# Banded attention: the sink as a score column, high parts of the memory weights on ScalarE, token-major sample values, and a third weight set for the output pair

## The reference, cut to what matters

```python
def sink_softmax(s, mask, sink):
    s = jnp.where(mask, s, -jnp.inf)
    sk = jnp.broadcast_to(sink.astype(jnp.float32), s.shape[:-1] + (1,))
    p = jax.nn.softmax(jnp.concatenate([s, sk], axis=-1), axis=-1)
    return p[..., :-1]
...
    s = jnp.einsum('nbqkgd,nbskd->nbkgqs', qb, kk, preferred_element_type=jnp.float32) * (HEAD_DIM ** -0.5)
...
    p = sink_softmax(s, mask[None, :, None, None], sink.reshape(KV_HEADS, GROUP)[None, None, :, :, None, None])
    o = jnp.einsum('nbkgqs,nbskd->nbqkgd', p.astype(vv.dtype), vv).reshape(n, t, Q_WIDTH)
...
def memory_kv(mem, g_mem, w_ck, w_cv):
    n, m = mem.shape[:2]
    mm = rmsnorm(mem, g_mem)
    mk = (mm @ w_ck).reshape(n, m, X_HEADS, X_HEAD_DIM)
    mv = (mm @ w_cv).reshape(n, m, X_HEADS, X_HEAD_DIM)
    return mk, mv
```

## Time and profile before

| | us |
|---|---|
| median of three timed runs | 2398.05 (2396.0 to 2401.09) |
| the profiled execution | 2398.91 |
| span of its trace | 2397.1 |
| mean granted TensorE clock | 0.981 |

### The profile page before, as it was taken

The page is one execution under the profiler, slowest core; times in us unless marked ns, Lnnn a source line. Parts: engine busy times, 40 slices in busy tenths (PEclk is TensorE's granted clock), DMA queues, the critical chain, the costliest instruction groups (busy, mean ns, idle before and its releaser), DMA issues.

```text
span 2397.1 us, 35513 instructions
## 1 busy us (share of the span) xinstructions
PE 2301.7 (96%) x14058; PEld 2066.1 (86%) x14058; DVE 1416.1 (59%) x1814; ACT 455.2 (19%) x924; POOL 1040.9 (43%) x703
## 2 busy tenths in 40 slices
PE   6999999999999999979899989999999999999997
PEld 5899989999989888867788967989999999999996
DVE  7755556555556677888525145375556565556565
ACT  5111000011000325345402034130000000000002
POOL 2643434343432256588354320535434343434333
PEclk9999999999999999989899999999999999999999
DMA  4201011101020211243311052122110111010102
GB/s 147 71 36 52 17 52 52 52 35 52 17 70 9 102 61 36 80 114 86 138 44 44 18 226 91 35 71 71 36 52 17 52 52 52 35 52 17 70 0 76
DMA packets 47781, 143.64 MB, mean 60 GB/s; under 512 B 7143, under 2 KB 17383, under 8 KB 45159
## 3 DMA queue, kind: packets, MB, share of 16 engines
q1 hardware_dynamic: 44768, 139.43, 16.8%
q10 hardware_dynamic: 2951, 3.35, 0.4%
HBM read 127.72 MB, written 12.26 MB: 58 GB/s over the span
## 4 chain that ended last, share of the span: by engine, by line
PE 88%; POOL 5%; DVE 3%; issue 2%; ACT 1%; DMA 0%; SPq 0%; POOLq 0%; ACTq 0%; DVEq 0%
PE ps L638 28%; PE ps L640 28%; PE ps L639 28%; PE ps L1088 1%; PE ps L1135 1%; POOL w_lo L534 1%; POOL kw_lo L534 1%; POOL w_hi L533 1%; POOL kw_hi L533 1%; PE ps L833 1%; DVE act_lo L1567 0%; POOL mix L591 0%; DVE y L2118 0%; PE ps L1095 0%; DMA x<-in_x 0%
## 5 line engine op out<-in xcount | busy, mean ns | idle before, releaser
L638 PE MATMUL ps<-act_hi,w_hi 128*128 128x288 f32 (+1 forms) x1968 | 658.5, 335 | 44.5 <-DVE act_lo L1567 23.6
L640 PE MATMUL ps<-act_hi,w_lo 128*128 128x288 f32 (+1 forms) x1968 | 650.6, 331 | 0.0
L639 PE MATMUL ps<-act_lo,w_hi 128*128 128x288 f32 (+1 forms) x1872 | 618.3, 330 | 0.0
L638 PEld LDWEIGHTS ps<-act_hi,w_hi 128*128 128x128 f32 x1968 | 375.2, 191 | 79.6 <-issue 44.3
L640 PEld LDWEIGHTS ps<-act_hi,w_lo 128*128 128x128 f32 x1968 | 375.4, 191 | 28.8
L639 PEld LDWEIGHTS ps<-act_lo,w_hi 128*128 128x128 f32 x1872 | 356.3, 190 | 28.8 <-issue 1.0
L1610 DVE SCALAR_TENSOR_TENSOR x<-ps,x 128x288 f32<-128x288 f32 (+1 forms) x504 | 263.4, 533 | 188.3 <-PE ps L640 173.0
L638 PE MATMUL ps<-hid_hi,dn_hi 128*128 128x288 f32 (+1 forms) x1056 | 347.5, 329 | 3.6 <-issue 3.6
L638 PE MATMUL ps<-act_hi,up_hi 128*128 128x288 f32 (+1 forms) x1056 | 347.7, 329 | 0.0
L639 PE MATMUL ps<-act_lo,up_hi 128*128 128x288 f32 (+1 forms) x1056 | 347.6, 329 | 0.0
L640 PE MATMUL ps<-act_hi,up_lo 128*128 128x288 f32 (+1 forms) x1056 | 347.6, 329 | 0.0
(11 more groups left out here) (264 smaller groups left out, 3021.8 us busy)
## 6 DMA issues: line engine op xcount, KB each, us to landing
w_raw<-in_w_ffn SPq DMA_DIRECT2D x66, 512.0 KB, 3.6
w_raw<-in_w_plain SPq DMA_DIRECT2D x54, 512.0 KB, 3.5
ff_raw_up<-in_w_ffn SPq DMA_DIRECT2D x44, 512.0 KB, 4.3
ff_raw_down<-in_w_ffn SPq DMA_DIRECT2D x22, 512.0 KB, 6.7
ck_T<-in_ck SPq DMA_DIRECT2D x8, 1024.0 KB, 7.0
cv_n<-in_cv SPq DMA_DIRECT2D x8, 1024.0 KB, 5.0
x_keep<-x SPq DMA_DIRECT2D x1, 4352.0 KB, 12.7
x<-x_keep SPq DMA_DIRECT2D x8, 544.0 KB, 5.2
```

What stands on the lines that cost most here:

```text
L638: pe.matmul(out, wh, ah, start=(first and n == 0), stop=False)
L639: pe.matmul(out, wh, al, start=False, stop=False)
L640: ins = pe.matmul(out, wl, ah, start=False, stop=end)
```

## The change

Six things are changed; what is computed stays the same.

1. The sink becomes column 257 of the scores (137 of the sample scores): set by a small copy (`set_sink`), it goes through the maximum and the exponentials with the others, and its share is in the sum. The separate exponential of the sink, the sum with it, and one step of the maxima go.
2. ScalarE makes the high parts of both slots for memory pairs from p = 2, and of slot 0 for p = 1 (`whi(p, s)`); GpSimd makes only low parts there.
3. The first memory pair: slot 0 is loaded before the wait for input tile 12 and split right behind the input pairs; slot 1 gets a set of its own (`kf_hi`/`kf_lo`), its load behind one swap load, and its product another PSUM bank. VectorE's third reciprocal of the recurrent group's norm moves behind the rotary of block 1.
4. The sample product gives token-major values: the weights are stationary in pieces of 32 columns and the values move. The result is copied by ScalarE (`so_T`) and turned back by TensorE in step 5 (`sample_back`); VectorE takes it in step 5, and the sample squares move from step 6 to 7.
5. The second output pair is split into a third set (`kx_hi`/`kx_lo`) when the last rotary and value transpose are done; the loop then covers pairs 2 and 3.
6. In the cross-attention the prompt product goes ahead of the sample product, with a semaphore of its own (`xp_ev`). ScalarE's `lru_hi` copies are spread over steps 5 and 6.

```diff
-        s_m = [here(f"s_m{s}", [P, NH, 2 * WIN]) for s in range(2)]
+        s_m = [here(f"s_m{s}", [P, NH, 2 * WIN + 1]) for s in range(2)]
...
+            def load_weights(p, s):
+                sp.wait_ge(w_split[s], p)
+                sp.dma_start(w_raw[s][:, :, :], pair_src(s, p)).then_inc(w_in[s], 16)
+
+            load_weights(PAIR_KV, 0)
             sp.wait_ge(lru_h, 4)
             sp.wait_ge(g_ev["in"], 6 + 13 * NC)
             load_swap(0)
+            load_weights(PAIR_KV, 1)
             load_swap(1)
-            load_pairs(PAIR_KV, PAIR_KV + 1)
             load_swap(2)
+            load_pairs(PAIR_KV + 1, PAIR_KV + 2)
...
-            split_pairs(1, PAIR_KV + 1, PAIR_IN, 0)
+            split_pairs(1, PAIR_KV, PAIR_IN, 0)
...
+            pool.wait_ge(w_mm[0], groups_before(PAIR_KV))
+            split_plain(0, PAIR_KV)
+            pool.wait_ge(ssq_mm, SUM0["lru"] + NC)
+            pool.wait_ge(lru_y, LT)
+            split_plain(1, PAIR_KV, [None, kf_hi], [None, kf_lo])
...
             for p in range(1, NB):
+                hi, lo = slots(kw_hi2[p % 2]), slots(kw_lo2[p % 2])
                 for s in range(2):
-                    if p == 1:
+                    if p == 1 and s == 1:
                         pool.wait_ge(w_mm[1], groups_before(PAIR_KV))
-                    elif s == 0:
-                        pool.wait_ge(kw_hi0, p - 1)
+                        split_plain(s, PAIR_KV + p, hi, lo, less=1)
                     else:
-                        pool.wait_ge(mem_mm, 2 * (p - 2) + 2)
-                    split_plain(s, PAIR_KV + p, p % 2, less=max(p - 1 - (s == 0), 0), both=p == 1 or s == 1)
+                        pool.wait_ge(kw_hi_made, 2 * (p - 1) + s if p > 1 else 1)
+                        split_plain(s, PAIR_KV + p, hi, lo, both=False)
...
+            pool.wait_ge(rope_done, NB)
+            pool.wait_ge(vt_mm, NB)
+            for s in range(2):
+                split_plain(s, PAIR_OUT + 1, slots(kx_hi), slots(kx_lo), less=less)
+            for s in range(2):
+                pool.wait_ge(w_mm[s], groups_before(PAIR_OUT + 1))
+                split_plain(s, PAIR_OUT + 2, less=less)
+            split_pairs(PAIR_OUT + 3, PAIRS, PAIR_OUT, 7 * NC, less=less)
...
-                for b in range(NS):
+                for h in range(2):
                     for kv in range(KVH):
-                        t, j = kv * 2 + b // 4, b % 4
-                        r = slice(kv * HD, kv * HD + HD)
-                        out = ps[r, 4, b * 32:(b + 1) * 32]
-                        pe.matmul(out, v_c[:, b, r], pcs_T[:, t, 32 * j:32 * j + 32], start=True, stop=False)
-                        ins = pe.matmul(out, vs_n[:, b, r], pns_T[:, t, 32 * j:32 * j + 32], start=False, stop=True)
+                        r, cols = slice(kv * HD, kv * HD + HD), slice(h * P + kv * HD, h * P + kv * HD + HD)
+                        for j in range(4):
+                            q = slice(32 * j, 32 * j + 32)
+                            pe.matmul(ps[q, 4, cols], pcs_T[:, kv * 2 + h, q], v_c[:, h * 4 + j, r], start=True, stop=False)
+                        for j in range(4):
+                            q = slice(32 * j, 32 * j + 32)
+                            ins = pe.matmul(ps[q, 4, cols], pns_T[:, kv * 2 + h, q], vs_n[:, h * 4 + j, r], start=False,
+                                            stop=True)
                 ins.then_inc(s_pv_mm, 1)
+
+            def sample_back():
+                pe.wait_ge(s_pt_ev, 4)
+                pe.wait_ge(pt_ev, 13)
+                for h in range(2):
+                    ins = pe.transpose(ps[:, 4, h * P:(h + 1) * P], so_T[:, h, :], ident[:, :])
+                ins.then_inc(s_back_mm, 1)
...
+            out_pair(1, kx_hi, kx_lo)
+            with pe.Fori(2, 4) as i:
+                out_pair(i, w_hi2, w_lo2)
...
             def x_weigh(b, half, s):
+                pe.wait_ge(xp_ev, b + 1)
+                pe.wait_ge(x_o_ev, b + 1)
+                for kt in range(KT):
...
-            def whi(p):
-
-                act.wait_ge(w_in[0], (PAIR_KV + p + 1) * 16)
-                act.wait_ge(mem_mm, 2 * (p - 2) + 2)
-                act.activation(kw_hi2[p % 2][:, 0, :, :], w_raw[0][:, :, :], ACT.Copy).then_inc(kw_hi0, 1)
+            def whi(p, s):
+
+                act.wait_ge(w_in[s], (PAIR_KV + p + 1) * 16)
+                if p == 1:
+                    act.wait_ge(w_mm[1], groups_before(PAIR_KV))
+                else:
+                    act.wait_ge(mem_mm, 2 * (p - 2) + 2)
+                act.activation(kw_hi2[p % 2][:, s, :, :], w_raw[s][:, :, :], ACT.Copy).then_inc(kw_hi_made, 1)
...
                 if b + 2 < NB:
-                    whi(b + 2)
+                    whi(b + 2, 0)
+                    whi(b + 2, 1)
...
+                if b == 4:
+                    act.wait_ge(s_pv_mm, 1)
+                    act.activation(so_T[:, :, :], ps[:, 4, 0:256], ACT.Copy).then_inc(s_pt_ev, 1)
...
                 steps.done(dve.tensor_reduce(st8[:, 0, :], scored(b)[:, :, :], AX_X, ALU.max))
-                steps.done(dve.scalar_tensor_tensor(out=st8[:, 1, :], in0=st8[:, 0, :], scalar=-(HD ** -0.5),
-                                                    in1=st8[:, 7, :], op0=ALU.mult, op1=ALU.min))
-                dve.tensor_tensor(st8[:, 2, :], st8[:, 1, :], c_("sink", 0, NH), ALU.add).then_inc(nmax_done, 1)
+                dve.tensor_scalar(st8[:, 1, :], st8[:, 0, :], -(HD ** -0.5), None, ALU.mult).then_inc(nmax_done, 1)
...
-                    steps.done(dve.tensor_tensor(st8[:, 5, h], st8[:, 3, h], st8[:, 4, h], ALU.add))
-                    steps.done(dve.reciprocal(st8[:, 6, h], st8[:, 5, h]))
+                    steps.done(dve.reciprocal(st8[:, 6, h], st8[:, 4, h]))
...
+            def set_sink(b, steps):
+                steps.done(dve.tensor_copy(scored(b)[:, :, 2 * WIN:2 * WIN + 1], st8[:, 7, :].unsqueeze(2)))
```

More of the change, by code:

```diff
@@ L230, in build @@
         vs_n = here("vs_n", [LS, NS, KVH * HD])
-        ss_m = here("ss_m", [P, 4, WIN + LS])
+        ss_m = here("ss_m", [P, 4, WIN + LS + 1])
         pcs_T = here("pcs_T", [P, 4, P])
         pns_T = here("pns_T", [LS, 4, P])
+        so_T = at("so_T", [P, 2, P], cur[0])
         qs_r = here("qs_r", [P, NS, GRP, LS])
@@ L564, in split_ffn, with split_plain @@
                 split_down(f, FI - 1)
-            def split_plain(s, p, v=0, less=0, both=True):
+            def split_plain(s, p, hi=w_hi, lo=w_lo, less=0, both=True):
                 pool.wait_ge(w_in[s], (p + 1) * 16)
                 steps = Steps(pool, w_pool, p * (2 * KT // SHORT) + s * (KT // SHORT) - less * (KT // SHORT))
-                split_short(w_raw[s], kw_hi2[v][:, s, :, :], kw_lo2[v][:, s, :, :], steps, w_split[s], both)
+                split_short(w_raw[s], hi[s], lo[s], steps, w_split[s], both)
             f = ffn["ffn1"]
@@ L1005, in block_step @@
                 if b == 5:
+                    pe.wait_ge(s_pt_ev, 4)
+                if b == 6:
                     pe.wait_ge(s_o_ev, 1)
@@ L1030, in block_step @@
                     sample_turn()
+                elif b == 5:
+                    sample_back()
                 if b + 2 < NB:
@@ L1064, in out_lo, with out_pair @@
                 return cat_lo[:, k, o:o + n] if k < LT else act_lo[:, k, o:o + n]
-            with pe.Fori(1, 4) as i:
+            def out_pair(i, hi, lo):
                 for s in range(2):
@@ L1124, in x_weigh @@
             def x_weigh(b, half, s):
+                pe.wait_ge(xp_ev, b + 1)
+                pe.wait_ge(x_o_ev, b + 1)
+                for kt in range(KT):
+                    for mt in range(2):
+                        ins = pe.matmul(ps[:, 6 + kt // 4, (kt % 4) * P:(kt % 4 + 1) * P],
+                                        mem_v[:, mt, kt * P:(kt + 1) * P], xp_T[:, mt, kt // 2, :],
+                                        start=(mt == 0), stop=(mt == 1))
+                ins.then_inc(x_pv_mm, 1)
                 pe.wait_ge(x_pt_ev, b + 2)
@@ L1937, in block_step @@
                     lru_lo(1)
+                if b + 2 < NB:
+                    set_sink(b + 2, steps)
                 if b + 1 < NB:
@@ L1962, in lru_inverse @@
                 dve.reciprocal(lru_rstd[:, o:o + n], lru_rstd[:, o:o + n]).then_inc(rstd_done, 1)
+            steps.done(dve.tensor_scalar(st8[:, 7, :], c_("sink", 0, NH), HD ** 0.5, None, ALU.mult))
+            set_sink(0, steps)
             lru_inverse(0)
@@ L1970, in _ @@
             take_in(13, [1])
-            lru_inverse(2)
-            steps.done(dve.tensor_scalar(st8[:, 7, :], c_("sink", 0, NH), -1.0, None, ALU.mult))
             dve.wait_ge(swa_tab, 16)
@@ L1977, in _ @@
             steps.done(dve.memset(v_n[1][:, :], 0.0))
+            set_sink(1, steps)
             rope(1, 1, steps)
+            lru_inverse(2)
             take_memory(0, 1)
```

86 lines of the change are left out of this document (44 added, 42 removed).

## The result

The changed kernel took 2356.09 us, median of 4 executions (2352.97 to 2359.17), against 2397.95 of the kernel before on the same chip: ratio 0.9823, 95% interval 0.9811 to 0.9835. Five more executions beside an experiment (2356.34 to 2358.53) put the median of all nine at 2357.4, 40.8 us under the 2398.2 of before there. Forecast: 2360, range 2352 to 2374, faster. The first profiled execution took 2354.55 us with a span of 2352.7; the second, of the same kernel, has a span of 2356.7. I read both, since they differ in just the place where the forecast is hardest to judge.

What follows compares the result with a forecast made beforehand. TensorE was taken to bound the kernel, so only its standing still or half clock could be won. Terms of 9.4, 4.5, 8.2, 1.0, 4.4, 0.2, 7.0 and 4.4 sum to 39.1; 2398.9 less that gives 2360 us, range 2352 to 2374.

Steps and rivals of the forecast that it cites:

- Start of the stage: From the start of the banded attention to block 1's weight transposes: earlier loads and splits win 9.4 us.
- T1 to T4: Weight transposes of block 1 to those of block 4: VectorE's saved small steps win 4.5 us, bounds 3.0 and 5.2.
- T4 to T5: Weight transposes of block 4 to block 5: sample product falls from 9.4 to 2.2 us; 8.2 us won.
- T5 to T6 and T6 to T7: Weight transposes of block 5 to 6, 1.0 us, mainly clock; 6 to 7, 4.4 us from waits and work gone.
- Behind T7: Behind block 7's weight transposes: 0.2 us won, bounds -1 and 3, the latter if the half clock goes too.
- Pair boundary: Ahead of and behind the second output pair: 5.36 us of wait and 1.7 of half clock go, 7.0 us won.
- cross-attention: TensorE's waits for `yp_T` go, as the prompt product moves ahead: 5.5 less 1.1 in the last block, 4.4 us.
- A: Rival: ScalarE stands behind the weights, 14.9 us a block against 12.6, 11 us over five blocks; 2371 us, chance 18%.
- D: Rival, slower: ScalarE behind the weights with dearest low parts, 22.3 us a block against 12.6; 2418 us, chance 3%.
- B: Rival: the sample product still drains at each product, 7.4 us in place of 2.2; 2365 us, chance 8%.
- C: Rival: start and blocks give less, through VectorE's queue and the score stride of 257; 2368 us, chance 8%.
- E: Rival: gains before block 7's weight transposes are swallowed by a later end that doesn't move; 2387 us, chance 1%.

Runs made afterwards that it cites:

- alternating order: The changed kernel with each 128-row product of the sample product followed at once by the 8-row product that adds to it: 2362.94 us.
- the old product: The changed kernel with the old sample product put back (values stationary, 32 probability columns moving, no copy or transposes back): 2364.73 us.
- the experiment: The changed kernel with slot 1's high parts of the memory weights made by GpSimd again from the third pair on: 2365.73 us.

## Why the prediction was right, and where not

- **What bounds the kernel**: right that TensorE and the engines that pace it do, too narrow in "only time in which TensorE stands still or runs at half clock can be won". The second largest term, the sample product, is work of TensorE itself that became shorter: 32 products at 0.23 are 7.4 us at the full clock, and they take 2.0 now. The prediction's own sum counts it so.
- **The signs.** The waits for `w_lo`, for `yp_T` and ahead of the second output pair are gone, and the sample product takes 2.0 us at clock 1.00, as told. One wait for `kw_lo` stayed, at the tile of 1033.05, whose start the prediction had; and the blocks are 12.4 to 15.1 us apart behind T1 and 10.8 before T7, not 12.5 to 13, since the sample work lies in some of them. GpSimd is busy 11.4 of 14 us, where about 10 a block were told.
- **Start of the stage, 9.4 predicted, 10.0 and 9.9 measured.** First memory tile without a gap (1018.36, predicted 1018.7); the tile of slot 1 of the second pair at 1033.05 (predicted 1033.5), T1 at 1047.2 (1048). The new wait of ScalarE for the load of the next slot 1 came as worked out: 4.15 us idle, then high part and take of the memory tile, until 1038.9. The 1.5 us that TensorE was to wait behind it did not come: in the first profile its tile at 1039.35 has no wait ahead, since it ran the tile of 1033.05 at the half clock until 1038.3; in the second it waited 0.6. The fear of the port between VectorE and GpSimd didn't come true in block 0: the multiply by the sines took 0.82, as with GpSimd idle in the earlier trace rows, because the split of slot 0 had ended before it. By the Trainium skill (SBUF — State Buffer, section Who interferes with whom) two such instructions block each other whole; block 1's multiply, beside a split, took 1.36 here, so the trace agrees in kind, and the rule had nothing to bite on in block 0.
- **T1 to T4, 4.5 predicted, 4.6.** The size is right in part by luck, since two errors nearly cancel. The copy of the sink column took 0.7 us in each of the three blocks and not 0.4, the upper end of its bounds (line L1927 of after: duration in ns, min/median/max, first and last start):

```profile
L1927 DVE COPY s_m<-st x7: 161/704/730, 1021.8 to 1111.1; 128x8 f32<-128x8 f32 x7
```

  In return the two small steps of the maxima took 1.2 a block before (3.7 in the three blocks) and the one in their place takes 0.4, a gain of 0.8 where 0.35 was counted. The stride of 257 costs nothing that shows: the reduction of 8 x 257 takes 2.29 as that of 8 x 256 did, an exponential of 257 columns 0.50 after 0.49.
- **T4 to T5, 8.2 predicted, 8.1.** The product took 2.0 (predicted 2.2), by another count: 8 groups at 0.25, with the further products in a group at almost nothing, where I had 0.03 each. The alternating order shows that this term rests on the changes of form. The Trainium skill (TensorEngine Tiling (Array Packing), section Key Properties) has the drain at a change of mode, and the trace agrees, with 0.23 us a change.
- **T5 to T6 and T6 to T7, 5.4 predicted, 5.6 in both profiles.** The 1.8 of half clock behind the sample product came back with the old product (1.8). But the price of the high parts was told too narrowly: 8 us by the experiment, not the 3.2 between T6 and T7. Each part's worth depends on the others being there: the prediction's terms by stretch are right, but they are not what each edit is worth.
- **Behind T7, 0.2 predicted, 4.1 in one profile and -0.4 in the other.** This is the term that the first profile seemed to refute, and its size there is not the change's: the same kernel had the half clock in the second profile. That the forecast is so near the median is in part luck, since this piece is worth 4.5 us either way. The bound of 3 for "the half clock goes too" was the right case and too small by 1. The sum of all pieces, 39.1, is 1.3 from the 40.4 of the second profile, and the 1.3 lie outside the pieces; against the median of nine the forecast is 2.6 us too slow.
- **Pair boundary, 7.0 and 7.1; cross-attention, 4.4 and 4.3 to 4.6.** Right, and shown by undoing each. In the cross-attention the 5.5 us for `yp_T` are gone; in the last block there are three waits of 2.2 together (0.2 before) and the wait ahead of the output projection is 0.9 shorter, which nets to the 1.1 that was left out.
- **The rivals.** A and D, ScalarE behind the weights in every block: false; it waits for a raw load 16.6 us in three places, 12.2 of it at the start of the stage and 4.2 in block 0, and in no later block. ScalarE's line L1384 in after, the high parts, sat idle before it until (us, times):

```profile
  DMA w_raw<-in_w_plain: 16.6, 3
```

  B, the drain at each product: false for the kernel and real for the other order. C, E and F: false.

## What to carry to other kernels

Group small products of one array form: four together (here on four different sets of 32 columns) cost what one costs, and the dense row of changing forms brought the half clock with it in the three profiles that have it. Where a step is cheap in itself, look at what stands behind it in its engine's order: the take of a memory tile held VectorE for 7.3 us, and eight exponentials held the copy that was to help GpSimd. Edits undone one by one tell that each matters, not what each is worth: two that serve one gain count it twice. Before a few us are credited to an edit, profile the unchanged kernel twice: a stretch whose clock goes either way can be worth more than the edit.

## What the hardware showed that I had not expected

- One kernel, the same waits in the same place (within 0.03 us), and clock 1.00 in one execution and 0.50 to 0.53 for ten us in another; worth 4.5 us. What decides it is open. It is not the length of the waits alone: with one wait of 0.70 the clock fell for 3.5 us, with waits of 0.47, 0.79 and 1.08 it stayed.
- The clock falls within a dense row of small products, without any gap: 4.7 us after the start of the alternating order, 2.5 us after that of the old product in the changed kernel and 3.3 in the kernel before.
- A change of form costs 0.23 us at the full clock and 0.35 at the half clock (the distance of the starts in the alternating order before and after 1104.9), and with four products between two changes still 0.25.
- VectorE's copy of 8 columns took 0.16 us in some places and 0.7 in most; what decides it is open.
